# Routing of an expert layer: slots and coefficients turned and spread by DMA, the top two picked tile by tile, seeds moved

## The reference

```
xn = RMSNorm(x)
group  = argmax over 4 of  xn @ rg_w + rg_b            # top-1 group, p_top its softmax share
le     = xn @ re_w + re_b, only the 8 experts of that group
top_l, top_i = the two largest of le                   # w_top = softmax(top_l) * p_top
out = sum over the two:  w_top * ( (silu(xn @ w_gate[e]) * (xn @ w_up[e])) @ w_down[e] )
y = RMSNorm(x + out)
```

## Time and profile before

| | |
|---|---|
| runs shown | 842.66 us median, 841.8 to 843.41 |
| the profiled execution's own time | 843.71 us, of which 841.9 are the span from the first to the last instruction |
| PE busy | 775.1 us (92%) |
| DVE, ACT, POOL busy | 427.0 (51%), 322.9 (38%), 262.6 (31%) |
| HBM traffic | 246.76 MB read, 2.75 written, 296 GB/s over the span |
| chain that ended last, by engine | PE 63%, DMA 18%, DVE 11% |

### The profile page before, as it was taken

One profiled execution on the slowest core, in us unless ns is written; L12 is line 12 of the kernel. 1 busy time (PEld: TensorE's weight loads), 2 busy tenths in 40 slices (PEclk: granted clock), 3 DMA queues, 4 the chain that ended last, 5 costly groups with the idle time before them and its releaser, 6 DMA issues.

```text
span 841.9 us, 21630 instructions
## 1 busy us (share of the span) xinstructions
PE 775.1 (92%) x8655; PEld 591.8 (70%) x8656; DVE 427.0 (51%) x1141; ACT 322.9 (38%) x560; POOL 262.6 (31%) x134
## 2 busy tenths in 40 slices
PE   4999999999999999999999988999998879979954
PEld 4999999999999999865555545555555545545532
DVE  3146977899994244153444433444433334434424
ACT  4533767564345833252322322322232213213223
POOL 3845699978677778200000000000000000000001
PEclk9999999999999999998999998999999999999997
DMA  7734343424454746973799999999999999999993
GB/s 244 238 102 149 101 144 107 151 100 153 137 173 154 292 150 226 339 292 151 313 424 421 423 422 422 422 422 422 422 423 421 422 422 422 422 422 422 421 422 142
DMA packets 53604, 249.99 MB, mean 297 GB/s; under 512 B 6647, under 2 KB 6647, under 8 KB 28993
## 3 DMA queue, kind: packets, MB, share of 16 engines
q1 hardware_dynamic: 50192, 246.96, 74.4%
q10 hardware_dynamic: 3377, 2.57, 1.2%
HBM read 246.76 MB, written 2.75 MB: 296 GB/s over the span
## 4 chain that ended last, share of the span: by engine, by line
PE 63%; DMA 18%; DVE 11%; SPq 3%; ACT 2%; issue 2%; ACTq 1%; DVEq 0%
PE bank L1465 24%; DMA piece<-in_exp_w_up 17%; PE bank L1636 13%; DVE bank L1079 7%; PE bank L1665 7%; PE bank L1587 5%; PE bank L1624 5%; PE bank L1463 4%; SPq L550 3%; PE bank L1652 1%; PE bank L1594 1%; DVE sq L1141 1%; DMA stage<-in_norm_g 1%; PE bank L1528 1%; ACT cvb L831 1%
## 5 line engine op out<-in xcount | busy, mean ns | idle before, releaser
L617 POOL TENSOR_TENSOR w_lo<-raw,w_hi 128x2048 fp32r<-128x2048 f32 x39 | 180.5, 4630 | 62.9 <-ACT w_hi L749 62.8
L1636 PE MATMUL bank<-piece,xe 128*32 128x256 f32 x2816 | 169.6, 392 | 32.6 <-DMA piece<-in_exp_w_up 26.9
L1636 PEld LDWEIGHTS bank<-piece,xe 128*32 128x32 f32 x2816 | 97.5, 113 | 99.3 <-issue 48.9
L1465 PE MATMUL bank<-x_hi,w_hi 128*128 128x384 f32 x432 | 145.4, 337 | 0.2 <-DVE ua L1098 0.2
L1465 PE MATMUL bank<-x_hi,w_lo 128*128 128x384 f32 x432 | 144.4, 334 | 0.0
L1465 PE MATMUL bank<-x_lo,w_hi 128*128 128x384 f32 x432 | 144.3, 334 | 0.0
L677 POOL TENSOR_SCALAR n_out<-n_out,small 128x512 f32<-128x512 f32 x2 | 3.6, 1790 | 447.1 <-DVE small L1350 447.1
L1079 DVE SCALAR_TENSOR_TENSOR bank<-ub,vec,bank 128x256 f32<-128x256 f32 (+1 forms) x416 | 137.1, 414 | 0.0
L749 ACT ACTIVATE w_hi<-raw 128x2048 fp32r<-128x2048 f32 x39 | 74.8, 1918 | 74.7 <-PE bank L1465 71.1
L1665 PE MATMUL bank<-piece,hidT 128*32 128x256 f32 x1408 | 94.2, 384 | 5.5
L1310 DVE SCALAR_TENSOR_TENSOR silu_and_hid<-bank,few,silu_and_hid 64x256 f32<-64x256 f32 x44 | 21.5, 490 | 140.4 <-ACT silu_and_hid L935 140.4
(11 more groups left out here) (241 smaller groups left out, 1032.0 us busy)
## 6 DMA issues: line engine op xcount, KB each, us to landing
piece<-in_exp_w_down SPq DMA_DIRECT2D x64, 1024.0 KB, 26.6
piece<-in_exp_w_gate SPq DMA_DIRECT2D x64, 1024.0 KB, 25.8
piece<-in_exp_w_up SPq DMA_DIRECT2D x64, 1024.0 KB, 26.9
raw<-in_w_in SPq DMA_DIRECT2D x28, 1024.0 KB, 5.2
raw<-in_w_out_a SPq DMA_DIRECT2D x4, 1024.0 KB, 5.0
raw<-in_w_out_b SPq DMA_DIRECT2D x4, 1024.0 KB, 5.1
raw<-in_w_o SPq DMA_DIRECT2D x4, 1024.0 KB, 5.0
out<-n_out SPq DMA_DIRECT2D x6, 256.0 KB, 2.2
```

The source lines that it names most:

```text
L617: pool.tensor_tensor(w_lo[u % NW][:, :, :], raw[u % NW][:, :, :], w_hi[u % NW][:, :, :].bitcast(F32), ALU.subtract).then_inc(lo_ready, 1)
L1465: ins = pe.matmul(b, wp[:, k % UK, cols], xp[:, k, :], start=start, stop=stop)
L1636: last = pe.matmul(GU[q * T:(q + 1) * T, :], xe[:, k, :], wide(pairs[q // 2], k)[:, q % 2 * QE:(q % 2 + 1) * QE], start=(k == 0), stop=(k ...
```

## The change

Three things in the routing, and what they need of semaphores:
- **Picking tile by tile.** DVE's picking is cut into steps of one tile, written out by hand in an order in which two tiles alternate. Each step waits only for the step before of its own tile. PE's counts of a tile wait for that tile's masks, and its first three seeds for one tile's logits each. The coefficients come right behind the masks, ahead of the reading of the counts.
- **Rows by DMA.** The columns of `values` are transposed in two parts, now first the coefficients with the norm's factor (12 rows), then the slots (6 rows). ACT's copy goes by DMA to a tensor in DRAM, `value_rows`, and SP loads it from there, each row to all partitions, into `spread_rows`. `spread`, its matmuls and ACT's copies of them are gone. Without them PSUM bank 2 is free.
- **Seeds.** `seed(0, 0)` stands ahead of `turn_rows` in place of behind the spreading. The order of the table's matmuls and of `turn_rows` is exchanged.

The diff, cut to its core:

```
-    AUX += [("pos", 0, "dve"), ("table", 0, "dve")]
-    AUX += [("turned", 0, "act"), ("spread", 0, "act"), ("spread", 1, "act"), ("order", 0, "dve")]
-    AUX += [("turned", 1, "act"), ("spread", 2, "act"), ("spread", 3, "act")]
+    AUX += [("pos", 0, "dve"), ("turned", 0, "act"), ("table", 0, "dve")]
+    AUX += [("turned", 1, "act"), ("order", 0, "dve")]
...
-        values = [scratch(3 * NT), scratch(2 * NT)]
-        slot_f = values[0][:, 0:2 * NT].rearrange("p (c i) -> p c i", c=2)
-        rstd2 = values[0][:, 2 * NT:3 * NT]
-        turned = [scratch(P, 3 * NT), scratch(P, 2 * NT)]
+        rank_of = scratch(NT)
+        sum_exp = scratch(NT)
+        values = scratch(6 * NT)
+        slot_f = values[:, 0:2 * NT].rearrange("p (c i) -> p c i", c=2)
+        rstd2, rstd2_too, coefs = values[:, 2 * NT:3 * NT], values[:, 3 * NT:4 * NT], values[:, 4 * NT:6 * NT]
+        turned = [scratch(P, 4 * NT), scratch(P, 2 * NT)]
+        value_rows = nc.dram_tensor("value_rows", (6 * NT, P), F32)
...
+            flat = spread_rows.rearrange("p c n -> p (c n)")
+
+            def rows_to_all(rows, r0, r1, c0):
+
+                sp.dma_start(flat[rows, c0:c0 + (r1 - r0) * P],
+                             value_rows[r0:r1, :].rearrange("(a r) p -> a (r p)", a=1)
+                             .to_broadcast([rows.stop - rows.start, (r1 - r0) * P])).then_inc(value_rows_in, 16)
+
+            sp.wait_ge(coefs_out, 16)
+            rows_to_all(slice(0, P // 2), 2 * NT, 4 * NT, 2 * N)
+            rows_to_all(slice(P // 2, P), 4 * NT, 6 * NT, 2 * N)
+            sp.wait_ge(slots_out, 16)
+            rows_to_all(slice(0, P), 0, 2 * NT, 0)
...
-            wait_aux_read(pool, aux("spread", 3))
+            pool.wait_ge(tables_ready, 1)
+            pool.wait_ge(value_rows_in, 48)
...
             read_aux(aux("turned", 0))
+            wait_aux_read(act, aux("turned", 0))
+            act.dma_start(value_rows[2 * NT:6 * NT, :], turned[0]).then_inc(coefs_out, 16)
+            read_aux(aux("turned", 1))
+            wait_aux_read(act, aux("turned", 1))
+            act.dma_start(value_rows[0:2 * NT, :], turned[1]).then_inc(slots_out, 16)
             copy_rows(1)
-            for a in ("spread", 0), ("spread", 1), ("turned", 1), ("spread", 2), ("spread", 3):
-                read_aux(aux(*a))
...
+            def best_group(i):
+                wait_aux_read(dve, aux("logit", i))
+                done(i, dve.tensor_reduce(gmax[:, i:i + 1], lg[:, i, 0:NG], AX.X, ALU.max))
+
+            def group_ranks(i):
+                ready(i)
+                done(i, dve.scalar_tensor_tensor(t0[:, i, 0:NG], lg[:, i, 0:NG], gmax[:, i:i + 1], down_rank[:, 0:NG],
+                                                 ALU.is_equal, ALU.mult))
+
+            def first_group(i):
+                ready(i)
+                done(i, dve.tensor_reduce(rank_of[:, i:i + 1], t0[:, i, 0:NG], AX.X, ALU.max))
...
+            read_logits(0)
+            best_group(0)
+            group_ranks(0)
+            first_group(0)
+            other_groups(0)
+            in_group(0)
+            best(0, 0)
+            ranks(0, 0)
+            first(0)
+            read_logits(1)
+            best_group(1)
+            mark_hot(0, 0)
...
+            read_logits(2)
+            best_group(2)
+            mark_hot(1, 0)
+            group_ranks(2)
...
+            ranks(2, 1)
             dve.tensor_tensor(dexp, top[1], top[0], ALU.subtract).then_inc(exp_in, 1)
-
+            first(2)
+            dve.wait_ge(exp_out, 1)
+            dve.tensor_reduce(sum_exp, gexp, AX.X, ALU.add).then_inc(dve_chain, 1)
+            chain[0] += 1
+            mark_hot(2, 1)
+            both_hot(2)
+            dve.wait_ge(exp_out, 2)
+            link(dve.scalar_tensor_tensor(inverse, dexp, 1.0, sum_exp, ALU.add, ALU.mult))
+            link(dve.reciprocal(inverse, inverse))
+            link(dve.tensor_tensor(coefs[:, 0:NT], inverse, rstd2, ALU.mult))
+            dve.wait_ge(rstd_ready, 2)
+            dve.tensor_tensor(coefs[:, NT:2 * NT], coefs[:, 0:NT], dexp, ALU.mult).then_inc(coefs_ready, 1)
...
-            wait_aux_read(pe, aux("logit", NT - 1))
+            wait_aux_read(pe, aux("logit", 0))
             seed(1, 0)
+            wait_aux_read(pe, aux("logit", 1))
             seed(1, 1)
+            wait_aux_read(pe, aux("logit", 2))
             seed(2, 0)
-            pe.wait_ge(masks_ready, 1)
             b = start_aux(aux("pos"))
+
             for i in range(NT):
+                pe.wait_ge(masks_ready, i + 1)
...
+            pe.wait_ge(coefs_ready, 1)
+            end_aux(pe.transpose(start_aux(aux("turned", 0))[0:4 * NT, 0:P], values[:, 2 * NT:6 * NT], ident[:, :]))
             seed(2, 1)
...
+            pe.wait_ge(slots_ready, 1)
+            end_aux(pe.transpose(start_aux(aux("turned", 1))[0:2 * NT, 0:P], values[:, 0:2 * NT], ident[:, :]))
...
-            pe.wait_ge(slots_ready, 1)
-            turn_values(0)
             pe.wait_ge(picked, 1)
             pe.wait_ge(x_rows_ready, NT)
             gather()
-            wait_aux_read(pe, aux("turned", 0))
-            spread(0)
-            spread(1)
-            pe.wait_ge(rows_ready, 1)
-            turn_rows()
             pe.wait_ge(order_ready, 2)
             b = start_aux(aux("order"))
             pe.matmul(b[0:1, 0:NE + 1], ones_b[0:NE, 0:1], up_to, start=True, stop=True)
             end_aux(pe.matmul(b[0:1, NE + 1:2 * NE + 1], number_b[:, :], at_place, start=True, stop=True))
-            pe.wait_ge(coefs_ready, 1)
-            turn_values(1)
-            wait_aux_read(pe, aux("turned", 1))
-            spread(2)
-            spread(3)
+            seed(0, 0).then_inc(combined, 1)
+            pe.wait_ge(rows_ready, 1)
+            turn_rows()
             pe.wait_ge(tables_ready, 1)
...
-            wait_aux_read(pe, aux("spread", 3))
-            seed(0, 0).then_inc(combined, 1)
```

More of the change, by code:

```diff
@@ L128, in trunk_program @@
     AUX_BANK = [4 + (a % 2 if aux("new") <= a <= aux("var") else a % 4) for a in range(len(AUX))]
-    for a, b in zip(range(aux("pos"), len(AUX)), (0, 1, 2, 1, 2, 1, 2, 1, 2)):
+    for a, b in zip(range(aux("pos"), len(AUX)), (0, 1, 1, 1, 1)):
         AUX_BANK[a] = b
@@ L738, in read_aux @@
                 elif name == "turned":
[L739 to L742, removed]
+                    act.activation(turned[j], b[0:turned[j].shape[0], 0:P], ACT.Copy).then_inc(act_aux, 1)
             def high_part(u):
@@ L914, in _ @@
             act.activation(zero[:, 2:3], zero[:, 0:1], ACT.Exp)
+            act.wait_ge(exp_in, 1)
+            act.activation(gexp, gexp, ACT.Exp).then_inc(exp_out, 1)
             act.wait_ge(exp_in, 2)
-            act.activation(gexp, gexp, ACT.Exp).then_inc(exp_out, 1)
             act.activation(dexp, dexp, ACT.Exp).then_inc(exp_out, 1)
@@ L1182, in _, with ready, done, read_logits @@
             dve.wait_ge(rstd_ready, 1)
-            for i in range(NT):
+            dve.tensor_copy(rstd2_too, rstd2).then_inc(rstd_ready, 1)
+            at = [0] * NT
+            def ready(i):
+                dve.wait_ge(dve_chain, at[i])
+            def done(i, ins):
+                chain[0] += 1
+                at[i] = chain[0]
+                ins.then_inc(dve_chain, 1)
+            def read_logits(i):
                 a = aux("logit", i)
@@ new lines, in in_group, with best, ranks @@
+            def in_group(i):
+                ready(i)
+                done(i, dve.tensor_tensor(le[:, i, :].rearrange("p (g e) -> p g e", g=NG),
+                                          lg[:, i, NG:R].rearrange("p (g e) -> p g e", g=NG),
+                                          t1[:, i, 0:NG].unsqueeze(2).to_broadcast([P, NG, EPG]), ALU.add))
+            def best(i, c):
+                ready(i)
+                done(i, dve.tensor_reduce(top[c][:, i:i + 1], le[:, i, :], AX.X, ALU.max))
+            def ranks(i, c):
+                ready(i)
+                done(i, dve.scalar_tensor_tensor(t0[:, i, :], le[:, i, :], top[c][:, i:i + 1], down_rank[:, 0:NE],
+                                                 ALU.is_equal, ALU.mult))
@@ new lines, in _ @@
+            mark_hot(0, 0)
+            group_ranks(1)
+            without_first(0)
+            first_group(1)
+            best(0, 1)
+            other_groups(1)
+            ranks(0, 1)
+            in_group(1)
+            first(0)
+            best(1, 0)
+            mark_hot(0, 1)
+            ranks(1, 0)
+            both_hot(0)
+            first(1)
+            read_logits(2)
+            best_group(2)
+            mark_hot(1, 0)
+            group_ranks(2)
+            without_first(1)
@@ new lines, in _ @@
+            first_group(2)
+            best(1, 1)
+            other_groups(2)
+            ranks(1, 1)
+            in_group(2)
+            first(1)
+            best(2, 0)
+            mark_hot(1, 1)
+            ranks(2, 0)
+            both_hot(1)
+            first(2)
```

(5 more changed lines are left out.)

67 lines of the change are left out of this document (21 added, 46 removed).

## The result

Measured side by side, the changed kernel took 837.39 us (835.12 to 838.42, 6 runs) and the kernel before 842.33 (841.51 to 843.41, 6 runs): a ratio of 0.9938, 95% interval 0.9923 to 0.9953. It is faster by 4.9 us, or 5.3 from the 842.66 that the prediction started from, where 7.2 were forecast (835.5); the time lies inside the range of 833.5 to 839.5. The profiled execution took 838.06 us, of which 836.3 are the span (before: 841.9).

The account below looks back on a forecast made before the run. The expert weight stream, whose start hangs on PE's item 3, was taken to set the end. 6.2 (spreading and seed, including 0.5 of picking) plus 1.0 (clock) gave 7.2 us: 835.5 from the median 842.66, range 833.5 to 839.5.

Parts of the forecast that it names:

- The stream's start sets the end: Unbroken expert weight stream from 418.62, released by PE's item 3: starting item 1 earlier reaches the end one for one.
- Gate and up of item 0 start 6.2 sooner: Between gather and expert loop: spreading by DMA and the moved seed start gate and up at 382.4, 6.2 us gained.
- Picking, 0.5 gained: DVE's routing masks: picking by tile ends them at 374.5 against 375.02, 0.5 us gained, counted within the 6.2.
- the prediction's bound: PE ahead of the position counts: three seeds end at 374.2, so picking can't gain over 0.9 us.
- The clock, 1.0 gained: Item 0's gate and up on PE: at the full clock 3.45 us instead of 4.45, 1.0 gained on top.
- The DMA rows cost nothing: Ahead of item 0's Silu: rows' chain ready at 385.5, before gate and up end at 385.85, so no cost.
- the two hops: Slots' rows stored to DRAM and loaded back on SP: 2.2 us each plus 0.3 for issuing, DMA being idle then.
- the 0.4 to spare: Slack of the rows' chain before gate and up's end; each microsecond of both hops beyond 4.8 costs one.
- a rival, with a chance of 0.12: Item 0's Silu waits for rows late by 1 to 4 us; at 3.5 us a hop 2.2 late, 837.7; chance 0.12.
- No draining behind a table load: ACT ahead of Silu: the skill's extra 1.38 us per table switch left out; with it, gain about 1 us smaller.

Follow-up runs that it names:

- control: The changed kernel with one more register operation (a max with 0) per loop bound on PE, base of the other experiments; first measured 836.94 us, ratio to before 0.9927.
- rows left out: Against the control, the slots' and coefficients' rows are not stored or spread by DMA; GpSimd fills them with zeros, nothing waits for them; 835.88 us, ratio 0.9913.
- weights held: Against the control, SP holds the three expert weight loads that follow the rows until all rows have landed; 835.67 us, ratio 0.9914.
- old picking: Against the control, the picking for all three tiles at once is put back, the rest stays changed; 838.43 us, ratio 0.9951.
- third seed later: Against the control, the third seed ahead of the position counts (tile 2's first half) goes behind the turns of the gathered rows; 835.01 us, ratio 0.9911.
- control again: The control unchanged, measured a second time, which gave the control's second profile; 837.75 us, ratio 0.9942.

## Why the prediction was right, and where its size was off

Step by step, in the times of the changed kernel's profile:

- **The stream's start sets the end:** right. Start and end moved alike (5.7 and 5.6), with an idle microsecond ahead.
- **Gate and up of item 0 start 6.2 sooner:** after the logits they start 5.6 sooner (22.3 to 16.8), and 6.6 in the control's second profile. From gather to gate and up it was 9.6 and is 3.65, 5.95 less, where the prediction had 5.8 (9.67 before against 382.4 - 378.5). Moving the seed has no part in that (put back, it changed nothing), but its clock has: the seed took 2.04 before and 1.12 now, so about 0.9 of the 5.95 is the full clock and the rest the spreading. The exchanged order of the table's matmuls and the turns was not tried by itself.
- **Picking, 0.5 gained:** the masks were (8.3 against 8.77; from tile 2's read, which came 0.8 later here, 3.95 against 5.27), and the 51 instructions overlap: where two tiles alternate they start mostly 0.10 to 0.16 apart, and each lasts 0.16 to 0.25 (371.03 and 371.19 above). By the rule of "VectorE: DVE Perf Modes" (Rules for kernel authors) on the number of operations, in the Trainium skill, they would have stood end to end; the trace is against that for instructions that don't need each other. But the prediction's bound, three seeds done by 374.2, took their duration from before. The clock was low from 367.5 to 374.4, not from 369.9 to 373.3, they took 5.38, and the counts came 0.5 later instead of 0.5 sooner. In the control's second profile the clock was low for 3.4 us again, and counts are read at 8.7, 0.7 sooner than before, within the bound of 0.9:

```profile
374.05 0.14 DVE L1335 COPY tmp<-bank 32x1 f32<-32x1 f32 x1
```

- **The clock, 1.0 gained:** right, a little less. It didn't fall again. In one and the same view, PE's timeline, gate and up of item 0 took 4.52 before (the line below) and 3.66 now, and item 1's take 3.64 (above). The 4.45 and 3.45 of the prediction are from the chain of waits, which counts a piece only from the end of the one before it (item 1 from 392.98, though its first matmul starts at 392.80). So item 1 is no faster than a first item at the full clock, and the term is 0.1 too large. Over the whole of item 0 it is 0.9 (9.9 before, 9.0 with the rows left out):

```profile
388.57 4.52 PE L1636 MATMUL bank<-piece,xe 128*32 128x256 f32 x64
```

- **The DMA rows cost nothing:** this is the step that failed. I put the two hops at 4.8 us with the issue, at the short end of the rows, because no weight load was in flight. They took 2.50 + 4.67 = 7.17. That is 2.4 beyond the 4.8, and less the 0.4 to spare 2.0: item 0 lasts 10.9 instead of the 9.0 that it has with the rows left out, 1.8 more. The mechanism was right (each microsecond beyond costs about one: with the weights held the hops take 5.8 and item 0 9.4), and it was a rival, with a chance of 0.12 and a price of 2.2 (837.7 us). So the measured 837.39 lies at that rival's time and not at the forecast's, whose own range ended at 836.8; it is in the stated range because that was widened for this rival. (The 4.8 is a slip by the prediction's own sum, too: hops of 4.7 and 0.35 to spare make 5.05, so two hops of 3.5 would cost 1.95.) The mis-sized term is the second hop. Its argument failed, too: the weight loads are issued 0.58 us behind it. In the nine profiles that have it the slots' load took 4.67, 4.15 and 4.74 with the weights 0.58 behind, 4.16 and 3.95 with 0.95, 3.3 with 1.02, 3.19 with 1.36, and 3.51 and 3.2 with the weights held. The Trainium skill, "DMA: Bandwidth & Descriptors" (Latency and other measured facts), has the latency of memory rise with its load; these rows fit that (4.67 beside the loads, 3.51 with them held), without telling the memory's latency from the sharing of the queue. Of the 2.4 us, then, 0.6 to 1.2 are the neighbours (4.15 to 4.74 in the three profiles with the weights 0.58 behind, against 3.51), and the rest the hops themselves. These are no constant either: with the old picking the store took only 1.4 and both hops 4.7, and why stays open.
- **No draining behind a table load:** right. The load at 386.62 lasts 1.28, and Silu starts at 387.91.

The sum of the trace: 5.95 for the spreading (with the seed's clock) and 0.87 for the clock in item 0, less 0.47 for the counts and 1.82 for the rows, 4.5; the work ahead of the routing ended 1.1 us sooner in this execution (365.11 against 366.25), which the change doesn't touch, and the two give the 5.6 of the span. That 1.1 is luck of the two executions; the medians are 4.9 apart.

## What to carry over

A transfer that replaces work on a busy engine is priced by its landing beside what is queued right behind it: ask what the next issue on that queue is, and hold that if it isn't urgent. Two dependent small transfers through DRAM took 4.7 to 7.2 us here, fine for values that are ready early (the coefficients) and too long for those ready last (the slots). And a duration taken from a stretch in which PE's clock was low is no constant: the same three seeds took 4.2 to 5.5 us.

## What the runs showed of the hardware beyond that

How long the clock is low behind the narrow logit matmuls differs between executions of one program: 3.4 us in the control's second profile and 6.8 in its first, worth 1.2 us at the gather (12.0 against 13.2). The length alone doesn't set it: "rows left out" has 3.4, too, and 13.0, for the reason given there. What starts it sooner or later stays open. "TensorE: Matmul & The Clock Gate" in the Trainium skill (Part 1: The HAM clock gate) calls the number of slow matmuls at a kernel's start variable between runs; these two profiles show the like in the middle of one.

The same shows at the end. From the chain of waits, the last expert's load and half of its gate and up, in the control's first and second profile:

```profile
787.54 25.99 DMA piece<-in_exp_w_up
813.67 3.29 PE bank L1718 x32
```

```profile
787.35 25.98 DMA piece<-in_exp_w_up
813.47 1.93 PE bank L1718 x32
```

The loads land 0.2 apart, but the spans are 835.3 and 833.4: in the first the clock was low at the last expert (3.29 instead of 1.93). Three of the profiles here have 1.93 (weights held, third seed later, control again), the others 2.9 to 3.6. From landing to the end it is 20.0 to 20.1 us in the one case and 21.5 to 22.9 in the other. That would be enough for much of the spread between executions of one kernel, which single profiles can't show, and it is a reason not to read medians closer than a microsecond. The profiles of the kernel before and of the changed one have 21.7 each, so their comparison is not touched by it. Nothing was tried against it.
